# A mixer that begins with its value projection, and reordered norm transitions, in a split-precision transformer kernel

## What is computed

```
g = norm_g[l]
h = swiglu_ffn(rmsnorm(x, g[0]), w_gate[l, 0], w_up[l, 0], w_down[l, 0])
x = x + 0.5 * rmsnorm(h, g[1])
h = hybrid_mixer(rmsnorm(x, g[2]), w_in[l], ...)
x = x + rmsnorm(h, g[3])
h = swiglu_ffn(rmsnorm(x, g[4]), w_gate[l, 1], w_up[l, 1], w_down[l, 1])
x = x + 0.5 * rmsnorm(h, g[5])
```

## Time and profile before

| what | value |
|---|---|
| median of 3 runs | 1520.59 us |
| profiled execution, device time | 1520.84 us |
| its span, first to last instruction | 1518.7 us |
| mean granted TensorE clock | 0.999 |
| HBM read | 256.7 MB, 170 GB/s |

### The profile page before, as it was taken

The page is one execution under the profiler, slowest core; times in us unless marked ns, Lnnn a source line. Parts: engine busy times, 40 slices in busy tenths (PEclk is TensorE's granted clock), DMA queues, the critical chain, the costliest instruction groups (busy, mean ns, idle before and its releaser), DMA issues. The chain is left out here.

```text
span 1518.7 us, 21963 instructions
## 1 busy us (share of the span) xinstructions
PE 1482.9 (98%) x9232; PEld 1300.2 (86%) x9232; DVE 970.2 (64%) x1195; ACT 712.4 (47%) x878; POOL 39.5 (3%) x50
## 2 busy tenths in 40 slices
PE   7999999999999999999999999999999999999998
PEld 6999999899988788888987888878888899878886
DVE  5767786587864656545876666456664568666644
ACT  4533863455543544445245444444444444454432
POOL 0000000000000000001010000000000010000000
PEclk9999999999999999999999999999999999999999
DMA  7635465566655566465323755547655543366542
GB/s 245 222 121 167 141 198 189 159 189 180 182 194 166 180 221 210 151 196 139 112 98 112 228 182 185 188 145 228 229 194 168 139 123 115 102 192 192 194 148 101
DMA packets 253461, 259.17 MB, mean 171 GB/s; under 512 B 26659, under 2 KB 217524, under 8 KB 253364
## 3 DMA queue, kind: packets, MB, share of 16 engines
q1 hardware_dynamic: 251424, 254.44, 52.8%
q10 hardware_dynamic: 1940, 3.33, 0.6%
HBM read 256.69 MB, written 1.05 MB: 170 GB/s over the span
## 5 line engine op out<-in xcount | busy, mean ns | idle before, releaser
L971 DVE TENSOR_TENSOR w_lo<-raw,w_hi 128x2048 fp32r<-128x2048 f32 (+1 forms) x240 | 545.3, 2274 | 335.7 <-ACT w_hi L589 335.5
L589 ACT ACTIVATE w_hi<-raw 128x2048 fp32r<-128x2048 f32 (+1 forms) x240 | 455.9, 1900 | 345.3 <-PE stream L1634 145.4
L1634 PE MATMUL stream<-a_hi,w_hi 128*128 128x256 f32 x1072 | 306.4, 286 | 4.3 <-DVE a_lo L1008 3.2
L1634 PE MATMUL stream<-a_lo,w_hi 128*128 128x256 f32 x1072 | 303.3, 283 | 0.0
L1634 PE MATMUL stream<-a_hi,w_lo 128*128 128x256 f32 x1072 | 303.2, 283 | 0.0
L1634 PE MATMUL stream<-w_hi,a_hi 128*128 128x512 f32 (+1 forms) x640 | 244.0, 381 | 6.4 <-DVE w_lo L971 6.4
L1634 PE MATMUL stream<-w_hi,a_lo 128*128 128x512 f32 (+1 forms) x640 | 239.3, 374 | 0.0
L1634 PE MATMUL stream<-w_lo,a_hi 128*128 128x512 f32 (+1 forms) x640 | 238.9, 373 | 0.0
L1634 PEld LDWEIGHTS stream<-a_hi,w_hi 128*128 128x128 f32 x1072 | 205.6, 192 | 7.5 <-DVE w_lo L971 3.9
L1634 PEld LDWEIGHTS stream<-a_lo,w_hi 128*128 128x128 f32 x1072 | 205.7, 192 | 0.0
L1634 PEld LDWEIGHTS stream<-a_hi,w_lo 128*128 128x128 f32 x1072 | 205.6, 192 | 0.0
(11 more groups left out here) (282 smaller groups left out, 1612.0 us busy)
## 6 DMA issues: line engine op xcount, KB each, us to landing
raw<-in_ffn_w_up SPq DMA_DIRECT2D x136, 512.0 KB, 5.0
raw<-in_ffn_w_down SPq DMA_DIRECT2D x104, 512.0 KB, 4.5
raw<-in_ffn_w_gate SPq DMA_DIRECT2D x88, 512.0 KB, 3.9
raw<-in_w_in SPq DMA_DIRECT2D x78, 512.0 KB, 4.6
raw<-in_w_out SPq DMA_DIRECT2D x24, 512.0 KB, 4.2
raw<-in_w_ret_o SPq DMA_DIRECT2D x8, 512.0 KB, 4.1
raw<-in_w_lru_o SPq DMA_DIRECT2D x8, 512.0 KB, 4.0
diag<-in_conv_diag SPq DMA_DIRECT2D x8, 512.0 KB, 5.8
```

Of the source, the lines that this page charges most:

```text
L589: nc.scalar.activation(w_hi[s][:, :, 0:n], raw[s][:, :, 0:n], ACT.Copy).then_inc(w_hi_ready, 1)
L971: V.tensor_tensor(w_lo[s][:, :, 0:n], raw[s][:, :, 0:n], w_hi[s][:, :, 0:n].bitcast(F32), ALU.subtract).then_inc(w_split, 1)
L1634: return nc.tensor.matmul(dst, lhs, rhs, start=start, stop=stop, skip_group_check=True)
```

## The change

It does these things.

- Start: unit 0 is loaded by SP, behind x; SP waits for unit 0's landing before it issues unit 1, and for unit 1's before unit 2. ACT issues positions, sink_row and the gate matrix behind hi(0).
- First block: lo(U1_UP + 1) and hi(U1_UP + 2) go behind tile 1's turned_lo and turned_hi; fillers 22 and 4 become 14 and 1; at the final norm x_square and next_variance of tile 0 go behind tile 1's norm, fillers 5 and 4 become 1 and 1.
- `tile_roots`: both post roots, then both pre roots. root_count follows.
- `between`: next_variance(0) goes behind the residual of tile 1; into a mixer lo(last + 2) and lo(last + 3) go behind both tiles' turned_lo, and hi(last + 3) behind x_square(1). Into an FFN hi(last + 3) goes ahead of x_square(0).
- Mixer: unit 0 is gla's value. Its tile-0 pass runs before turn(1), its tile-1 pass behind. Units glr, qk, ca, cg, kv, q, q move up by one number; r stays 8. No fillers.
- Mixer's order: lo(cm + 4) and lo(cm + 5) together; hi(cm + 4) ahead of the log-sigmoid; ACT's read of the value at the front; hi(cm + 10) ahead of the second exponentials; taps on DVE (0-4, 4-6, 6-9, 9-17, 17-22, 22-27, 27-29, 29-31) and on PE (3, 2, 4, 6, 6, rest) distributed anew; the output's statistics ahead of probabilities(0).
- FFN: turn_hidden of pair 0 behind pass (3, 0) instead of (2, 1).

```
 fill:        if c >= NS:
                  sp.wait_ge(w_split, c - NS + 1)
-             for dst, src in halves(raw[s]) if c else ():
+             elif c:
+                 sp.wait_ge(raw_loaded[c - 1], 32)
+             for dst, src in halves(raw[s]):
 tile_roots:
-                for t in range(TT):
-                    if post:
-                        inverse_root(rs4[:, t:t + 1], var4[:, t:t + 1], 1)
-                    if pre:
-                        inverse_root(rs4[:, 2 + t:3 + t], var4[:, 2 + t:3 + t], 1)
+                for at in [0, 1] * post + [2, 3] * pre:
+                    inverse_root(rs4[:, at:at + 1], var4[:, at:at + 1], 1)
 dve, first FFN:
             add_half(U1_OUT + 2, 1, 0)
-            lo(U1_UP + 1)
             add_half(U1_OUT + 3, 1, 1)
             two_halves(2, 1, 4, RMS_EPS)
             scaled(1)
+            turned_lo(N_UP1, 1, 0, V1["norm2"])
+            lo(U1_UP + 1)
             lo(U1_UP + 2)
-            turned_lo(N_UP1, 1, 0, V1["norm2"])
 dve, between:
-                lo(last + 2)
-                if group is not None:
-                    next_variance(i, 0, next_eps)
+                to_mixer = group is not None and col
+                if not to_mixer:
+                    lo(last + 2)
                 two_halves(0, 1, squared + 4, 4 * RMS_EPS)
                 at[1].append(gained(1, 1, squared + 4))
                 residual(i, 1, at[1])
-                lo(last + 3)
+                if not to_mixer:
+                    lo(last + 3)
                 if group is not None:
+                    next_variance(i, 0, next_eps)
                     turned_lo(i, 1, group, col)
                     next_variance(i, 1, next_eps)
+                if to_mixer:
+                    lo(last + 2)
+                    lo(last + 3)
 pe, ffn:
-                    if t == 1 and m == 0 and g:
+                    if (j, t) == (3, 0) or t == 1 and m == 0 and g > 1:
                         turn_hidden(f, g - 1)
 pe, mixer:
-                spin(psm[:, 0, :], 19)
-                turn(i, 1, x_t)
-                spin(psm[:, 2, :], 4)
...
                 unit(0)
-                end_pass(feature_major(cm % NS, bank(0), BOTH[0:1], a_hi, a_lo, True, True,
-                                       ready=a_ready(i, 1)), cm)
+                token_major(cm % NS, bank(0), 0, UC, 0, True, (0,), a_ready(i, 0))
+                turn(i, 1, x_t)
+                end_pass(token_major(cm % NS, bank(0), 0, UC, 0, True, (1,), a_ready(i, 1)), cm)
+                unit(1)
+                end_pass(feature_major((cm + 1) % NS, bank(1), BOTH[0:1], a_hi, a_lo, True, True), cm + 1)
...
-                unit(7)
-                token_major((cm + 7) % NS, bank(7), 0, 256, 0, True, (0,))
-                window_scores(1)
-                end_pass(token_major((cm + 7) % NS, bank(7), 0, 256, 0, True, (1,)), cm + 7)
                 unit(8)
                 first_half(8)
-                pe.wait_ge(group_evac, gm + 8)
+                window_scores(1)
+                second_half(8)
                 psm_ready(PSM_L)
...
-                second_half(8)
+                conv_taps(4)
```

More of the change, by code:

```diff
@@ L62 @@
 TOTAL_UNITS = U1_END + LAYERS * UL
-QUERY_UNITS = [U1_END + UL * l + UL_MIX + 5 + n for l in range(LAYERS) for n in range(2)]
+QUERY_UNITS = [U1_END + UL * l + UL_MIX + 6 + n for l in range(LAYERS) for n in range(2)]
 G1_RG = 20
@@ L86 @@
 HELD = 3
-GATE_UNITS = [U1_END + UL * l + UL_MIX for l in range(LAYERS)]
+GATE_UNITS = [U1_END + UL * l + UL_MIX + 1 for l in range(LAYERS)]
 TAP_SLOT = (0, 1, 2, 3, 16, 17, 18, 19, *range(4, 16), *range(20, 31))
@@ L874, in turned_probabilities @@
                     ins.then_inc(pt_free, 1)
+                act.wait_ge(unit_used, USED[cm])
+                act.wait_ge(rstd_ready, root_count(N_L + 3 * l, False, 1))
+                for t in range(TT):
+                    ins = nc.scalar.activation(vg[:, t, :], stream[gm % 3][:, t * T:t * T + T], ACT.Identity,
+                                               scale=rs4[:, 2 + t:3 + t])
+                ins.then_inc(group_evac, 1)
                 hi(cm + 3)
+                hi(cm + 4)
                 act.wait_ge(ps7_full, ps70 + PS7_Z + 1)
@@ L896, in _ @@
                 nc.scalar.activation(s_cross[:, :, :], psm[:, :, 0:P], ACT.Copy).then_inc(psm_free, 1)
-                hi(cm + 8)
+                hi(cm + 9)
                 exponentials(0)
[L899 to L905, removed]
+                hi(cm + 10)
                 exponentials(1)
@@ L1665, in _, with token_major @@
             BOTH = [(block_cols(0), 0), (block_cols(1), T)]
-            def token_major(s, dst, col, width, at, begin, tiles=range(TT)):
+            def token_major(s, dst, col, width, at, begin, tiles=range(TT), ready=None):
                 for t in tiles:
@@ L2035, in _ @@
                 first_half(4)
-                gla_scores(0)
                 second_half(4)
@@ L2039, in _ @@
                 first_half(5)
+                gla_scores(0)
+                second_half(5)
+                unit(6)
+                first_half(6)
                 gla_scores(1)
-                second_half(5)
-                pe.wait_ge(group_evac, gm + 5)
+                second_half(6)
+                pe.wait_ge(group_evac, gm + 6)
                 pe.wait_ge(ps7_free, ps70 + PS7_V)
@@ L2082, in _ @@
                 conv_taps(6)
+                pe.wait_ge(og_sq, l + 1)
+                pe.wait_ge(gla_free, 2 * l + 1)
+                for t in range(TT):
+                    for f in range(2):
+                        at = 4 * t + 2 * f
+                        ins = mm(gla_out[:, at:at + 2], cols(sq2[:, f, :], t), headsel, at == 0, at == 6)
+                ins.then_inc(stat_full, 1)
                 probabilities(0, [psm[:, m, :] for m in range(3)])
@@ L2099, in _ @@
                 cbank = stream[2]
-                pe.wait_ge(og_sq, l + 1)
-                pe.wait_ge(gla_free, 2 * l + 1)
-                for t in range(TT):
-                    for f in range(2):
-                        at = 4 * t + 2 * f
-                        ins = mm(gla_out[:, at:at + 2], cols(sq2[:, f, :], t), headsel, at == 0, at == 6)
-                ins.then_inc(stat_full, 1)
                 conv_taps(6)
```

131 lines of the change are left out of this document (66 added, 65 removed).

## The result

| | before | after |
|---|---|---|
| device time, median of 4 runs | 1520.62 us | 1496.97 us (1496.73 to 1498.52) |
| profiled execution, device time | 1520.84 us | 1498.52 us |
| its span | 1518.7 us | 1496.4 us |
| mean granted TensorE clock | 0.999 | 0.997 |

The ratio is 0.9847, with a 95% interval of 0.9835 to 0.9859: 23.65 us less where 25.1 were forecast. The time on record was 1495.5, 1.5 us too low. The profiled execution is the slowest of the four, so where its parts are compared the gain is 22.3 us.

The account below looks back on a forecast made before the run. Bound: PE's instruction stream plus PE's idle time. 3.0 + 2.9 + 1.7 + 12.4 + 3.7 + 1.4 = 25.1 us off 1520.84 gives 1495.7, the median 0.25 lower, 1495.5; own range 1492 to 1499, stated range 1490.5 to 1502.

Parts of the forecast that it names:

- 1, start: Start: with vec_rows no longer behind 1 MB of weights, vectors turn at 10.45 instead of 13.49; 3.0 us.
- 2, into the first FFN: First block's FFN: weight splits moved behind let the residual's last add and the first product come earlier; 2.9 us.
- 3, final norm: First block's final norm: with x_square and a second root behind, the norm and lo(U1_END+2) finish earlier; 1.7 us.
- 4 and 5: Mixers' front: shorter chain, value's first-tile pass in its shadow, 6.2 us a mixer, 12.4 for two; tail: DVE keeps up, 0.
- 6, hidden turn: FFNs: turning the hidden pair one pass later removes PE's waits for hb at four turn_hidden and their refilling; 3.7 us.
- 7, post roots first: Three transitions into an FFN: one root less ahead on POOL, 0.45 us each, 1.4 us.
- The clock rival: Clock falls where fillers went (U1_UP, final norm, both mixers): next 24 matmuls cost 2.95 us more each, 1507.3; chance 0.04.
- Granted clock 1.00 from there on: Expected sign at the start: clock at full rate from vec_rows' turn at 10.5 onward.
- a clock row below 1 after 20 us: Sign that the prediction is wrong: granted clock below full rate in the changed profile after 20 us.
- the rival that gave the tail to DVE: Mixers' tail: p_ready or the convolution sum comes late, 3 us of each mixer come back, 1501.5; chance 0.09.
- The splits one unit later: Mixers: lo(cm+3) ends 706.4 against 709.2; rival: lead lost, 12 waits of 4.2 us, 50 us, 1545.9, chance 0.02.
- The start's rival: Start gives nothing: two queues share the bandwidth and vec_rows still lands near 13; 1498.5, chance 0.10.

Follow-up runs that it names:

- experiment 2: Also written b_nofill: the kernel before without the 19 and 4 fillers ahead of each mixer, nothing else; 1525.32 us, ratio 1.0033.
- experiment 5: Also written a_nocover: the changed kernel with the value's tile-0 pass behind tile 1's transposes instead of ahead, at both mixers; 1502.57 us.
- experiment 11: Also written a_minus: the changed kernel with the old start and the old place of turn_hidden; 1504.55 us, ratio 0.9893.
- a_better: The changed kernel with lo(cm + 7) behind gla_scores(0) on DVE and unit 6's second half behind the transposes of the window's value; 1494.26 us.
- a_startfill: The changed kernel with 22 instead of 14 fillers at the start; 1497.63 us, ratio 0.9849.
- b_start: The kernel before with only the changed loading at the start (`fill` and ACT's queue); 1517.72 us, ratio 0.9983.
- b_hidden: The kernel before with only turn_hidden of pair 0 moved behind pass (3, 0) in the four FFNs; 1516.33 us, ratio 0.9974.
- b_roots: The kernel before with post roots first and tile 0's next_variance behind tile 1's residual, in every transition and the final norm; 1517.46 us.
- the spread kernels: a_better with each group of score matmuls issued in two halves between a unit's matmuls, 1494.03 us; the same with 22 start fillers, 1493.54 us.
- a_again: The changed kernel run again, unchanged; 1497.9 us, ratio 0.9846.
- a_oldsplits: The changed kernel with the weight splits of the mixer's second and third unit back in their old places; 1499.21 us, ratio 0.9864.

## Why the prediction was right, and where it was not

| term | forecast | measured |
|---|---|---|
| 1, start | 3.0 | 3.28 to the gates here; 2.8 alone |
| 2, into the first FFN | 2.9 | 2.77 |
| 3, final norm | 1.7 | 1.75 |
| 4 and 5, first mixer | 6.2 | 6.29 |
| 4 and 5, second mixer | 6.2 | 2.69 |
| 6, hidden turn | 3.7 | 4.2, alone |
| 7, post roots first | 1.4 | 1.4 |
| sum | 25.1 | 22.3 profiled, 23.65 by medians |

**The step that failed** is the second mixer's 6.2. It was priced as twice the first, since the code is the same, and the chains are: only PE's stand inside the scores (2.1 us with what it costs to start again) and the half-rate stretch behind it (1.5) differ, together the 3.5 us missing. In the kernel before, those scores ran without a stand, and nothing in its trace warned of one. The start (0.3) and the hidden turns (0.5) gave a little more than forecast, so the profiled execution is 2.8 us short of the sum. The other three runs, at 1496.73 to 1497.2, are 1.3 to 1.8 us below it, with a mean clock of 0.998 for 0.997; that they lost less to the clock fits, but they have no trace. The median is 1.5 short, and 2.0 over all nine executions. The sum had no term for a stand that no engine causes.

**A sentence that was wrong, with little harm here.** "A filler taken out is worth nothing by itself: the chain behind it ends when it ends." The chain does end when it ends, but the matmuls behind it run at half rate. Alone, taking the mixers' fillers out cost 4.8 us (experiment 2). The clock rival had the mechanism right and its places wrong: at both mixers it came true where only the fillers went (experiment 2), 2.3 a pass instead of its 2.95, since at half rate the 24 matmuls took 5.26 us, 1.8 times their 2.95 and not twice. In the changed kernel it did not, because the change puts 24 real matmuls where 19 fillers were; with these moved away it came at one mixer of two (experiment 5). At U1_UP and the final norm, where fillers went and nothing took their place, the stands were 0.8 to 1.3 us and the clock stayed at 1.00. I gave the shadow's use its price and saw the clock as a thing apart.

**"Granted clock 1.00 from there on"** was wrong at the start. It fell at about 16.8 to 1.2 GHz, behind 3.3 us of fillers and a wait of 1.79. What I wrote of it, that PE then runs at DVE's pace, held here: the stretch from the first product to the recurrence's gates lasted 134.45, as before. In three kernels where the fall came at 18.6 to 18.7 the stretch lasted 135.2, for then PE had begun on the full pass. So the start's term depends on when the clock falls, by 0.7 us. The prediction also named "a clock row below 1 after 20 us" as a sign of being wrong, and it came, at 1228.46.

**A bound that does not come out.** The prediction's own range starts at 1492, but the terms that it gives for that end, 1.0 at the start and 0.4 at each front, make 1493.7. Nothing that was measured hangs on it.

**What held.** The tail: DVE kept up at 5.94 us less of PE, with 1.7 us at the last sum for the 1.4 forecast, and the rival that gave the tail to DVE had no wait in its favour. The splits one unit later: no w_lo wait at units 2 to 8. The start's rival fell by vec_rows at 10.46. And the terms were taken separately and added; experiment 11 shows that to be allowed for the start and the hidden turns.

**The stand's cause.** All seven profiles with the mixer's new order and the scores in one piece have it: five with 1.26 to 1.80 us in the second mixer, a_better with 0.62 there, a_startfill with 1.48 in the first. With the scores cut in two there was none, nor in before, b_start, b_hidden and b_roots. It is not tied to the scores: in b_nofill PE stood 0.82 us among the large matmuls behind them. It is tied to a place in PE's instruction stream. The columns below count PE's matmuls and weight loads up to the stand in after, b_nofill and a_startfill:

```profile
0.00:1227.40 1227.40, 1206.18 (x7750) 1069.90 (x7750) 805.43 (x988) 596.72 (x721) 30.08 (x42) 1.00 0.57 179
```
```profile
0.00:1250.79 1250.79, 1214.73 (x7750) 1075.36 (x7751) 803.84 (x987) 594.34 (x718) 31.90 (x42) 0.99 0.56 175
```
```profile
0.00:729.26 729.26, 714.79 (x5006) 657.56 (x5006) 494.14 (x611) 364.75 (x428) 14.89 (x24) 1.00 0.59 184
```

PE's trace has 7750 matmul records ahead of it in every kernel with the stand in or behind the second mixer's scores, although that point came anywhere between 1223.94 and 1250.79 us. With PE's recorded waits counted in, it is instruction 15,810 (15,809 in b_nofill), and in a_startfill instruction 10,178, which is 22 times 256 earlier. The trace also has loads on a queue of kind "instruction"; here is the page's line on it, and that for 1224 to 1229 in the changed kernel:

```profile
q8 instruction: 72, 1.18, 0.3%
```
```profile
q8 instruction: 2, 0.03, 2.7%
```

That is 72 packets of 16 KB for the 18,595 instructions recorded for PE, one for every 258. In all eight stands the last such packet had landed 1.3 to 1.5 us before PE went on. So what the traces show is a stand at the end of a block of 256 instructions, where the last packet had only just arrived; the spread kernels pass the same instruction, inside their scores, with the packet landed 4.0 and 5.2 us earlier, and do not stand. That late instructions are the cause is an inference from this. Why the packet is late there stays open: how fast 256 instructions are used up does not settle it, for the kernel before used two such blocks in 4.00 and 4.87 us, one after the other, at 728 to 737, and did not stand. No run moved the block's end on purpose.

## What to carry to other kernels

Look for chains in whose shadow PE runs fillers, and move real work there; where PE would stand some 5 us without them, the fillers may go only if that work takes their place, since alone they were worth 2.4 us each time; ahead of the first FFN and at the final norm, where stands of 0.8 to 1.3 us are left, they went for nothing. Where a part is used twice, check the second place in the trace rather than doubling the first, and read the line "issue" among the waits: PE can stand for 2 us for no reason in the code. If it does, count its instructions up to the stand and look at the "instruction" queue. Spreading the tiny matmuls among larger ones took the stand away here, but cost 0.68 us a mixer, so that it gained nothing clear of noise over a_better.

## What the runs showed that I had not expected

- **Standing and the clock.** The length of a stand did not decide whether the clock fell behind it. At 1.80 us it fell in one profile of the changed kernel and not in the other (after, a_again), at 1.83 in the first mixer and not in the second (a_oldsplits), at 2.47 likewise (a_nocover); one of 1.53 lowered it (a_nocover, in the scores) and one of 1.55 did not (a_minus). Those of 1.3 us and less left it at 2.4 GHz, but for the start, where it fell behind 1.3 to 1.8; 5.12 lowered it both times (b_nofill). Where it fell behind one of the stands from 1.53 to 2.47, it did so 0.5 to 1.1 us after PE had gone on, and at the start of the changed kernel likewise: the stretch of 13.00 to 16.00 with 1.21 us of PE busy had 1.00, and the fall came at 16.7.
- **Half rate costs less than twice.** Over the 24 matmuls of a pass it was 2.3 us more on 2.95 (b_nofill), and nothing where DVE fed PE (the start).
- **A stand that belongs to the program.** The same 1.80 us between the same two score matmuls in two profiled executions of one kernel, and at the same count of PE's instructions, or 22 blocks of 256 earlier, in six other kernels.
